# Reordering the held weight tiles and the next stage's weight splits in a Transformer kernel's norm stages

## The reference

```python
x = x + einsum('bsd,de->bse', merged, w_merge_out)       # block 1: mixers, merged
h = rms_norm(x, ffn_norm)
x = x + einsum('bsf,fd->bsd', silu(h @ w_gate) * (h @ w_up), w_down)
x = x + nsa_mixer(rmsnorm(x, norm_mix_w), ...)           # block 2
x = x + memory_cross_attention(rmsnorm(x, norm_cross_w), mem_n, ca_wq, ca_wkv, ca_wo)
x = x + conv_ffn(rmsnorm(x, norm_ffn_w), ...)
return rmsnorm(x, final_norm_w)
```

## Time and profile before

| | |
|---|---|
| median of three runs | 1792.64 us |
| span of the profiled execution | 1789.8 us |
| TensorE busy | 1719.5 us, 96% of the span |
| VectorE, ScalarE, GpSimd busy | 960.8, 837.0, 961.6 us |
| mean granted clock of TensorE | 0.989 of full speed |
| HBM read | 156.09 MB, 88 GB/s over the span |

### The profile page before, as it was taken

The page is one execution under the profiler, slowest core; times in us unless marked ns, Lnnn a source line. Parts: engine busy times, 40 slices in busy tenths (PEclk is TensorE's granted clock), DMA queues, the critical chain, the costliest instruction groups (busy, mean ns, idle before and its releaser), DMA issues.

```text
span 1789.8 us, 27394 instructions
## 1 busy us (share of the span) xinstructions
PE 1719.5 (96%) x10334; PEld 1521.6 (85%) x10334; DVE 960.8 (54%) x1636; ACT 837.0 (47%) x1665; POOL 961.6 (54%) x701
## 2 busy tenths in 40 slices
PE   6999999999999999999989999999899899999998
PEld 4898887888877998999868978888788789989996
DVE  2246555453538751674138469984133388518842
ACT  4234554233335651554346358873443456426642
POOL 2354332334435774786336459972752358648852
PEclk9999999999999999999989999999999999999999
DMA  6332221223342333233324330002441223323331
GB/s 225 89 84 55 71 68 49 58 63 100 106 165 71 95 124 101 74 116 124 88 77 145 107 95 1 26 13 71 145 126 60 71 70 108 113 88 95 115 122 47
DMA packets 222899, 162.07 MB, mean 91 GB/s; under 512 B 9768, under 2 KB 197296, under 8 KB 222768
## 3 DMA queue, kind: packets, MB, share of 16 engines
q1 hardware_dynamic: 221712, 159.26, 29.7%
q10 hardware_dynamic: 1056, 1.06, 0.2%
HBM read 156.09 MB, written 2.11 MB: 88 GB/s over the span
## 4 chain that ended last, share of the span: by engine, by line
PE 39%; DVE 5%; issue 3%; ACT 2%; POOL 1%; DVEq 0%; ACTq 0%
PE psum L365 12%; PE psum L367 12%; PE psum L366 12%; DVE nprobL L2720 2%; DVE stat L2713 1%; PE psum L2634 1%; POOL w_low L352 1%; DVE oT L2731 0%; PE psum L2650 0%; PE psum L2649 0%; ACT w_high L344 0%; PE psum L449 0%; PE psum L2312 0%; DVE x L438 0%; PE psum L2622 0%
## 5 line engine op out<-in xcount | busy, mean ns | idle before, releaser
L352 POOL TENSOR_TENSOR w_low<-ring,w_high 128x1024 fp32r<-128x1024 f32 (+2 forms) x223 | 484.2, 2175 | 606.4 <-ACT w_high L344 605.9
L365 PE MATMUL psum<-hT,w_high 128*128 128x512 f32 (+1 forms) x1072 | 375.2, 350 | 9.5 <-PEq L184 6.4
L344 ACT ACTIVATE w_high<-ring 128x1024 fp32r<-128x1024 f32 (+2 forms) x223 | 212.2, 955 | 367.5 <-PE psum L367 367.4
L366 PE MATMUL psum<-hL,w_high 128*128 128x512 f32 (+1 forms) x1072 | 369.3, 345 | 0.0
L367 PE MATMUL psum<-hT,w_low 128*128 128x512 f32 (+1 forms) x1072 | 369.2, 344 | 0.0
L365 PEld LDWEIGHTS psum<-hT,w_high 128*128 128x128 f32 x1072 | 205.6, 192 | 32.3 <-issue 6.6
L367 PEld LDWEIGHTS psum<-hT,w_low 128*128 128x128 f32 x1072 | 205.1, 191 | 24.5
L366 PEld LDWEIGHTS psum<-hL,w_high 128*128 128x128 f32 x1072 | 205.5, 192 | 21.4
L1784 POOL TENSOR_TENSOR w_low<-ffn_sums,w_high 128x512 fp32r<-128x512 f32 x120 | 170.9, 1438 | 50.7 <-ACT w_high L1779 50.4
L1784 POOL TENSOR_TENSOR w_low<-ring,w_high 128x512 fp32r<-128x512 f32 x120 | 155.4, 1297 | 59.0 <-ACT w_high L1779 52.2
L365 PE MATMUL psum<-ffn_th,w_high 128*128 128x256 f32 x640 | 181.6, 284 | 4.9 <-DVE ffn_g L2018 3.3
(11 more groups left out here) (441 smaller groups left out, 3750.9 us busy)
## 6 DMA issues: line engine op xcount, KB each, us to landing
ring<-in_w_in SPq DMA_DIRECT2D x58, 512.0 KB, 3.6
ring<-in_ffn_w_up SPq DMA_DIRECT2D x44, 512.0 KB, 3.9
ring<-in_w_gate SPq DMA_DIRECT2D x22, 512.0 KB, 3.7
ring<-in_w_up SPq DMA_DIRECT2D x22, 512.0 KB, 4.8
ring<-in_w_down SPq DMA_DIRECT2D x20, 512.0 KB, 3.8
ring<-in_ffn_w_down SPq DMA_DIRECT2D x20, 512.0 KB, 3.9
ring<-in_nsa_w_in SPq DMA_DIRECT2D x18, 512.0 KB, 3.6
ring<-in_ca_wkv SPq DMA_DIRECT2D x16, 512.0 KB, 3.8
```

Source lines behind the costliest of these rows:

```text
L344: nc.scalar.activation(tile_view(w_high, n, SPLIT), tile_view(ring, n, RING), ACT.Copy).then_inc(w_hi, 1)
L352: nc.gpsimd.tensor_tensor(tile_view(w_low, n, SPLIT), tile_view(ring, n, RING), tile_view(w_high, n, SPLIT), ALU.subtract).then_inc(w_lo, 1)
L365: nc.tensor.matmul(ps, lhsT=sh, rhs=mh, start=first, stop=False)
L366: nc.tensor.matmul(ps, lhsT=sh, rhs=ml_, start=False, stop=False)
```

## The change

It has four parts.

1. **TensorE, in all five norm stages:** after token tile 0's matmuls with H1 and H2, it makes token tile 1's matmuls with H1, and then those of token tile 0 with H3. Token tile 1 goes on with H2 and H3.
2. **ScalarE, in the four norm stages that have a next stage:** W2's high part is taken right after W1's, before token tile 3's square, and W3's ahead of token tile 3's `high_part`.
3. **ScalarE, in the attention output stage:** H3's high part is taken before `memT` instead of after it.
4. **TensorE, in the key tiles:** the last turn comes after key tile 0 instead of after key tile 1.

```diff
--- before.py
+++ after.py
@@ -591,13 +591,20 @@
                         if held and between is not None:
                             pe.wait_ge(out_v, tiles)
                             between["pe"](pe)
+                        def held_tile(t, s):
+                            wh, wl = tile_for(pe, n0 + s, wname)
+                            for kk in range(plan[n0 + s][2]):
+                                mm = products(s, kk, wh, wl, t)
+                            if t == tiles - 1:
+                                mm.then_inc(w_used, 1)
+                            return mm
+
                         for t in range(tiles if held else 0):
-                            for s in range(per - held, per):
-                                wh, wl = tile_for(pe, n0 + s, wname)
-                                for kk in range(plan[n0 + s][2]):
-                                    mm = products(s, kk, wh, wl, t)
-                                if t == tiles - 1:
-                                    mm.then_inc(w_used, 1)
+                            for s in range(per - held + (t == 1), per):
+                                if t == 0 and s == per - 1:
+
+                                    held_tile(1, per - held)
+                                mm = held_tile(t, s)
                             if t < tiles - 1:
                                 mm.then_inc(tile_done, 1)
                             if t >= 1 and not store:
@@ -654,9 +661,9 @@
                         for t in range(tiles):
                             a.wait_ge(out_v, t + 1)
                             norm.square(a, t, 0, BANK)
+                        split_high(a, n0 + per)
                         if between is not None:
                             between["a"](a)
-                        split_high(a, n0 + per)
                         for t in range(tiles):
                             a.wait_ge(out_v, tiles + t + 1)
                             norm.square(a, t, BANK, BANK)
@@ -664,8 +671,8 @@
                             if t >= 1 and not store:
                                 norm.high_part(a, t - 1)
                             if t == tiles - 2:
-                                split_high(a, n0 + per - min(SPLIT, per) + SPLIT + 1)
-                        split_high(a, n0 + per - min(SPLIT, per) + SPLIT + 2)
+                                split_high(a, n0 + per - min(SPLIT, per) + SPLIT + 2)
+                        split_high(a, n0 + per - min(SPLIT, per) + SPLIT + 3)
                         if not store:
                             norm.high_part(a, tiles - 1)
                     if ahead is not None:
@@ -2808,7 +2815,7 @@
 
         def last_norm_turn(pe, i):
 
-            if i == 2:
+            if i == 1:
                 norm2.turn(pe, NT - 1)
 
         def after_out(pe, i):
```

## The result

The changed kernel takes 1798.14 us, the median of ten runs (1795.93 to 1799.66). The kernel before, beside it on the same chip, took 1792.65 us (1790.74 to 1795.34, ten runs). The ratio is 1.0029, with a 95% interval of 1.0020 to 1.0038: slower by 5.5 us. The prediction was 1799.1 us, range 1788.5 to 1802.5, with a chance of 0.65 on slower. The span of the profiled execution grew from 1789.8 to 1795.0 us, TensorE's mean granted clock went from 0.989 to 0.982, and VectorE's busy time rose from 960.8 to 971.8 us with the same number of instructions.

The account below looks back on a forecast made before the run. TensorE, busy 96%, bounds the kernel except at the very end, where VectorE's norm chain does. 3.6 + 3.6 + 2.8 + 1.4 - 6.7 = +4.7, plus 1.8 for the clock: 1792.6 + 6.5 = 1799.1 us, range 1788.5 to 1802.5.

Parts of the forecast that it names:

- Part 1: H1 ahead of H3: 0 in merge and cross attention, 1.36 us later in the first FFN and at the end.
- rival D: Merge and cross attention: the gap before H3 is a whole gain, 1.4 us each; 1796.3 us; 0.15 with a smaller collision.
- parts 1 and 3 in the attention output: Attention output: H3 starts sooner and the next turn waits less; 1.2 us gained up to key tile 0, between 0.4 and 1.55.
- The hold: Token tile 3's `L438` halves held by W2's and W3's `w_low`: +3.6 us each in merge and cross attention's output.
- Rival A: VectorE isn't held in `L438` beside a `w_low`: 1785.2 us, chance 0.12.
- rival B: VectorE is held once only, both `L438` halves going before W3's low part: 1788.9 us, chance 0.11.
- C: W3's low part goes before even the first `L438` half: another 0.3 us a stage; forecast including it, chance 0.62.
- First FFN: First FFN's end: VectorE ends the stage instead of GpSimd, +2.8 us with part 1's 1.36 us inside.
- Key tiles: Attention output and key tiles: 9.0 us from gaps and clock, less 2.3 for the held `L438`: 6.7 us gained.
- The clock: New gaps before the first FFN's turn and in the key tiles' last turn: 0 to 1.7 us each, 0.9 taken.

Follow-up runs that it names:

- after: The changed kernel with all four parts of the change, timed beside the kernel before: 1798.14 us, ratio 1.0029.
- parts 1, 3 and 4 together: The changed kernel without part 2 (W2's and W3's high parts at their old places): 1786.56 us, ratio 0.9972 to the kernel before.
- part 1 alone: The kernel before with only token tile 1's H1 ahead of token tile 0's H3 in all five norm stages: 1792.94 us, ratio 1.0003.
- the short low parts: The changed kernel with W2's and W3's low parts behind each norm stage computed for only 8 of each 128 columns: 1783.66 us, ratio 0.9955.
- W3's alone short: The changed kernel with only W3's low part behind each norm stage computed for 8 of each 128 columns: 1788.29 us, ratio 0.9976.
- parts 2 and 4: The kernel before with W2's and W3's high parts earlier and the last turn behind key tile 0: 1795.32 us, ratio 1.0021.
- part 4 alone: The kernel before with only the last turn moved behind key tile 0: 1784.20 us, ratio 0.9953.
- part 2 alone: The kernel before with only W2's and W3's high parts earlier in four norm stages: 1792.92 us, ratio 1.0005.
- the two kernels that take only what pays: Kernel before with paying edits only: 1782.66 us; that plus moved table load and part 1 in merge and cross attention: 1778.56 us.

## Why the prediction was right, point by point

- **Part 1.** Merge and cross attention: 0 forecast, +0.2 and +0.1 measured alone; the gap moved to the turn (1.57 us), so rival D is out. First FFN and end: 1.36 each forecast, 1.4 each measured. For parts 1 and 3 in the attention output 1.2 us were counted, and 1.2 were measured, in after as in parts 1, 3 and 4 together; with part 1 alone it was 0.7.
- **The hold.** The merge stage was to lose 3.6 us and lost 3.3 at its mark, the cross attention's output 3.6 and lost 3.4. The second half of `L438` was put at 548.75 and ended at 548.70. Rival A falls with the short low parts, rival B with W3's alone short, and C with the rows: W3's `w_low` came between the halves, not ahead of them. The Trainium skill's page "SBUF — State Buffer", section "SBUF: two separate sides", goes further than the page I used: an instruction that got the port pair shared by VectorE and GpSimd keeps it to its end, and the other engine stands still. The rows agree: `L438` ends 0.55 us behind the `w_low`, and the `w_low` beside it keeps its length (2.48 us, alone 2.36), so one engine stands and the two don't share. That the two take turns where both have work queued is shown by these runs (1.35 us, then 2.03).
- **First FFN.** 2.8 us and 0.9 for the clock forecast, 3.7 measured. The clock did fall behind the 2.25 us (894.14, eight transposes in 1.94 us and not 1.23), and cost 1.1.
- **Key tiles.** 6.7 us gain less 0.9 for the clock forecast, 6.6 measured, with the clock up behind the 2.03 us. The sum is right. How I built it was loose: I gave the 1.84 us to part 2 and the 4.20 to part 4, and did not see that each alone takes nearly all of the gain (6.6 and 6.2).
- **The clock.** 0.9 for each of two new gaps: one fell, one didn't. As a price for a coin that was fair, and that the sum came out is in part luck; part 1 alone and parts 2 and 4 show the same two gaps with the coin the other way up.
- **What I left out.** The second FFN. Its first gap is between 1.06 us (part 4 alone) and 2.16 (before), with the clock falling or not, and no edit touches it. In after it gave 0.2 us, so the sum held, by luck: 5.2 in the spans for 6.5 forecast, 5.5 in the medians. With the 2.7 us that it gave beside part 1 alone, the change would have cost about 3 us.

The 1.3 us between the 6.5 of the forecast and the 5.2 of the spans are 0.8 at the key tiles, where the clock term of 0.9 did not come, and 0.3 and 0.2 by which the holds in the merge and cross attention stages were put too high.

Still open: why the second FFN's gap meets GpSimd as it does. The traces show that it turns on less than 0.2 us between the starts of the two engines' operations, and nothing here steered it on purpose. Part 3 was not run alone; the 0.5 us between part 1 alone and parts 1 and 3 in the attention output is all that the runs show of it.

## What to carry to other kernels

An operation taken earlier on one engine can land its follower beside work that it holds up: before GpSimd's split is moved ahead, look at which two-input operations VectorE then has in its window, and who waits for them. Two edits that remove the same gap are worth it once, so time each alone and both together. An effect of a few microseconds far from the edit, like the second FFN's 2.7, says nothing of the edit's own mechanism: add the stages up by the rows' starts before explaining a median, and see how far the profiled execution lies from it.

## What the hardware showed that I had not expected

The length of a gap doesn't say whether TensorE's clock falls to half. Behind 1.77 or 1.78 us in the second FFN it fell in after, in part 2 alone, in parts 2 and 4 and with both low parts short, and stayed up with W3's low part alone short and in the two kernels that take only what pays. Behind 2.25 us in the first FFN it fell in after and with both low parts short, and not in the four other kernels with that gap. Behind 2.03 and 2.04 us in the key tiles it fell once of two. A fall cost 1.1 us in the first FFN (token tile 2's square came that much later still than token tile 0's) and 1.6 in the second. They may be part of the 3.7 us (after) and 4.6 us (before) by which the runs of one kernel differ; no run here parts that out.
